# Output projection and second norm of the last head pair begun inside its attention steps

## The reference

```python
s = einsum('bqhd,bkhd->bhqk', q_c, k_c) * scale + bias      # per chunk of 64, 9-chunk band
p = softmax(where(valid, s, NEG)); o = einsum('bhqk,bkhd->bqhd', p, v_c)
x = x + o @ w_o                                              # 16 heads of 64, width 1024
h = x * rsqrt(mean(x*x) + EPS) * g                           # second norm (ln_ffn)
a = h @ w_up                                                 # 1024 -> 2 * 2816
c = conv_b + sum_j full[:, j:j+T] * conv_w[j]                # causal, width 3
gate, val = split(c); x = x + (silu(gate) * val) @ w_down
```

## Time and profile before

| | us |
|---|---|
| median of 3 runs (2596.01 to 2598.01) | 2596.25 |
| profiled execution, its own time | 2593.85 |
| its span | 2592.3 |
| TensorE busy in the span | 2515.1 (97%) |
| VectorE busy | 1560.4 (60%) |
| ScalarE busy | 877.2 (34%) |
| GpSimd busy | 232.0 (9%) |

### The profile page before, as it was taken

How to read it: one execution, slowest core, us unless ns; L and a number is a source line. 1 busy time by engine, 2 the same in 40 slices (tenths; PEclk the granted TensorE clock), 3 DMA queues, 4 the chain that set the end, 5 groups by cost and what they waited for, 6 DMA issues and landing times.

```text
span 2592.3 us, 44046 instructions
## 1 busy us (share of the span) xinstructions
PE 2515.1 (97%) x16343; PEld 2426.8 (94%) x16343; DVE 1560.4 (60%) x2978; ACT 877.2 (34%) x1647; POOL 232.0 (9%) x521
## 2 busy tenths in 40 slices
PE   7999999998899999999999999999999999999998
PEld 7888888886799999999999899999999999999998
DVE  4566666566766666666666624244666666666666
ACT  5433334434522222233332531233333332222223
POOL 0000000000400000000000421222000000000003
PEclk9999999999899999999999999999999999999999
DMA  6111111110111111111111110111111111111012
GB/s 150 47 35 45 41 48 41 39 34 23 33 49 33 49 49 49 49 49 49 49 49 33 51 49 17 41 43 49 49 49 49 49 49 49 49 37 44 32 49 77
DMA packets 101512, 121.32 MB, mean 47 GB/s; under 512 B 3900, under 2 KB 90084, under 8 KB 101412
## 3 DMA queue, kind: packets, MB, share of 16 engines
q1 hardware_dynamic: 97892, 109.91, 13.2%
q0 software_dynamic: 2864, 7.88, 1.3%
q10 hardware_dynamic: 656, 2.12, 0.2%
HBM read 109.49 MB, written 10.40 MB: 46 GB/s over the span
## 4 chain that ended last, share of the span: by engine, by line
PE 89%; DVE 4%; ACT 3%; POOL 2%; issue 1%; DMA 0%; ACTq 0%; DVEq 0%; POOLq 0%
PE psum L160 26%; PE psum L162 26%; PE psum L161 26%; PE psum L906 3%; PE psum L886 3%; PE psum L871 2%; POOL total L231 2%; PE psum L1708 1%; DVE gx_lo L219 1%; PE psum L779 0%; ACT w_hi L679 0%; ACT conv_t L1392 0%; DVE x L1131 0%; DVE gx_lo L1867 0%; DVE conv_t L1457 0%
## 5 line engine op out<-in xcount | busy, mean ns | idle before, releaser
L160 PE MATMUL psum<-gx_hi,w_hi 128*128 128x352 f32 x3264 | 1069.4, 328 | 22.9 <-DVE w_lo L1282 10.6
L161 PE MATMUL psum<-gx_lo,w_hi 128*128 128x352 f32 x3264 | 1058.1, 324 | 0.0
L162 PE MATMUL psum<-gx_hi,w_lo 128*128 128x352 f32 x3264 | 1057.5, 324 | 0.0
L160 PEld LDWEIGHTS psum<-gx_hi,w_hi 128*128 128x128 f32 x3264 | 617.4, 189 | 29.7 <-issue 13.3
L161 PEld LDWEIGHTS psum<-gx_lo,w_hi 128*128 128x128 f32 x3264 | 617.7, 189 | 0.9 <-issue 0.7
L162 PEld LDWEIGHTS psum<-gx_hi,w_lo 128*128 128x128 f32 x3264 | 617.4, 189 | 0.0
L1484 DVE TENSOR_TENSOR x<-x,psum 128x352 f32<-128x352 f32 x528 | 259.1, 518 | 122.3 <-PE psum L162 122.3
L1392 ACT ACTIVATE conv_t<-a_gate,cur 128x352 f32<-128x352 f32 x132 | 90.2, 683 | 534.7 <-DVE a_gate L1449 534.4
L160 PE MATMUL psum<-h_hiA,w_hi 128*128 128x352 f32 x528 | 172.7, 327 | 4.3 <-DVE x L1484 4.3
L160 PE MATMUL psum<-h_hiB,w_hi 128*128 128x352 f32 x528 | 172.7, 327 | 0.0
L162 PE MATMUL psum<-h_hiB,w_lo 128*128 128x352 f32 x528 | 172.2, 326 | 0.0
(11 more groups left out here) (187 smaller groups left out, 3233.1 us busy)
## 6 DMA issues: line engine op xcount, KB each, us to landing
raw<-in_f_w_up SPq DMA_DIRECT2D x44, 1024.0 KB, 5.1
raw<-in_f_w_down SPq DMA_DIRECT2D x22, 1024.0 KB, 4.9
raw<-in_a_w_qkv SPq DMA_DIRECT2D x24, 512.0 KB, 3.8
raw<-in_b_w_in SPq DMA_DIRECT2D x8, 1024.0 KB, 5.8
raw<-in_a_w_o SPq DMA_DIRECT2D x8, 512.0 KB, 3.6
raw<-in_b_w_out SPq DMA_DIRECT2D x4, 1024.0 KB, 5.2
out<-raw SPq DMA_DIRECT2D x6, 512.0 KB, 2.7
xin<-in_x_prompt SPq DMA_DIRECT2D x4, 512.0 KB, 8.4
```

The costliest lines, as they stand in the source:

```text
L160: pe.matmul(out, w[0], rhs[0], start=first, stop=False)
L161: pe.matmul(out, w[0], rhs[1], start=False, stop=False)
L162: return pe.matmul(out, w[1], rhs[0], start=False, stop=last)
```

## The change

- The first six pairs are written out in place of the loop, on every engine.
- The maxima of the two heads are two reductions, and each exponential waits for its own.
- In the last pair all 24 tiles of the pair before stand in passes 0 to 3, and the last pair's own 24 in passes 5 to 10 (`LATE_WO` gives for each pass the tiles ahead of and behind the middle of it). Passes 0 to 3 use banks 7 and 3 in turn, passes 4 to 8 bank 7 alone, passes 9 and 10 four banks.
- In passes 4 and 5 the first gate unit of the FFN is split; from pass 6 on tiles of the second norm are done in the passes (`NORM_TILES`).
- `rstd` comes in two parts (blocks 0 to 3; the rest), in functions of their own. The first FFN iteration of the first layer takes its first six items as (0,0), (1,0), (0,1), (1,1), (0,2), (1,2) in (u, c).
- Buffers are laid out anew so that the FFN's first value weights can be loaded once the pair before the last is through.

The diff, cut:

```diff
+    LATE_WO = [(3, 4), (3, 4), (3, 4), (3, 0), (0, 0), (1, 2), (1, 2), (0, 2), (1, 2), (3, 2), (0, 8)]
...
+            LATE_BANK[late_m] = (7, 3)[late_m % 2] if late_s < 4 else 7 if late_s < STEPS else late_m % 4
+    def late_free(m):
+        return max([j for j in range(m) if LATE_BANK[j] == LATE_BANK[m]], default=-1) + 1
+    NORM_TILES = {6: range(0, 2), 7: range(2, 4), 8: range(4, 6), 9: range(6, 10)}
...
+        def late_wo(s, part):
+            for m in late_tiles(s, part):
+                t, n = LAST - 1 + m // BURST, m % BURST
+                at_least(pe, at_added, ADDED0 + BURST * (LAST - 1) + late_free(m))
...
+                wo_tile(pe, n, t, LATE_BANK[m], O_LAST if m >= BURST else O_MAIN)
...
-                if late and s < STEPS:
-                    turn(t, s - 1, third)
-                    if s >= 4:
-                        late_wo(t, s, 0)
-                    late_wo(t, s, 1)
+                if late:
+                    if 4 <= s < STEPS:
+                        late_wo(s, 0)
+                    turn(t, s - 1, third)
+                    late_wo(s, 1)
...
-        with pe.Fori(0, PAIRS // 2 - 1) as j:
-            pair(2 * j, 0)
-            pair(2 * j + 1, 1)
+        for t in range(LAST - 1):
+            pair(t, t % 2)
...
             for h in range(2):
-                if h == 0:
-                    act.wait_ge(max_done, STEPS * t + s + 1)
+                act.wait_ge(max_done, 2 * (STEPS * t + s) + h + 1)
...
+                if late and s == STEPS:
+                    for m in NORM_TILES[s]:
+                        norm.act_tile(act, *divmod(m, KT))
                 if 1 <= s <= STEPS:
                     copy(t, s - 1, range(min(2, len(key_groups(s - 1)))))
...
-        ffn[0].split(act, None, 0, 0)
-        for c in range(NCH):
-            for d in range(KT):
-                norm.act_tile(act, c, d)
+        for m in range(LAST_NORM, 2 * KT):
+            norm.act_tile(act, *divmod(m, KT))
         act.wait_ge(wo_done, 1 + BURST * PAIRS)
+        ffn[0].split(act, None, 0, 1)
+        for d in range(KT):
+            norm.act_tile(act, 2, d)
...
-            dve.tensor_reduce(neg_max[:rows_of(s), :], both_scores(s), AX.XY if n > BANK else AX.X, ALU.max,
-                              negate=True).then_inc(max_done, 1)
+            for h in range(2):
+                dve.tensor_reduce(neg_max[:rows_of(s), h:h + 1], scores_of(s, h), AX.XY if n > BANK else AX.X, ALU.max,
+                                  negate=True).then_inc(max_done, 1)
...
                     scale(t, s)
                     if late:
+                        late_adds(s, 1)
+                        if s == 5:
+                            ffn[0].split(None, dve, 0, 0)
+                        for m in NORM_TILES.get(s - 1, ()):
+                            norm.dve_tile(dve, *divmod(m, KT))
...
+                elif late:
+                    for m, tile in zip(late_tiles(s, 1), range(NORM_TILES[9][0], LAST_NORM + KT)):
+                        add(LAST, m % BURST, LATE_BANK[m])
+                        norm.dve_tile(dve, *divmod(tile, KT))
...
+        def items(self, first):
+            plain = [(u, c) for u in range(4) for c in range(NCH)]
+            if not first or self.layer:
+                return plain
+            return [(u, c) for c in range(NCH) for u in range(2)] + plain[2 * NCH:]
...
+                    if first and self.layer == 0:
+                        if o in (4, 6):
+                            nb_columns(pe, (o - 4) // 2)
+                        elif o in (5, 7):
+                            nb_spreads(pe, ((0,), (1, 2))[(o - 5) // 2])
...
+                    if first and o == 0 and self.layer == 0:
+                        nb_roots(act, 0)
+                        nb_rstd(act, (0,))
+                        act.wait_ge(self.up, 2 * NCH - 1)
+                        self.split(act, None, it, 2)
+                    elif first and o == 2 and self.layer == 0:
+                        nb_roots(act, 1)
+                        nb_rstd(act, (1, 2))
...
+    def raw1_over(engine):
+        engine.wait_ge(pv_done, 2 * STEPS * LAST)
+        engine.wait_ge(kv_turned, KV_FIRST + KV_PAIR * LAST)
+        engine.wait_ge(v_out, 32 * LAST)
```

More of the change, by code:

```diff
@@ new lines, in nb_roots, with nb_spreads @@
+    def nb_roots(act, g):
+        for k, (rows, cut) in enumerate(NB_COLS[g]):
+            act.wait_ge(nb_mean, NB_AT[g + 1])
+            act.activation(rs_col[rows, cut], rs_col[rows, cut], ACT.Sqrt).then_inc(nb_root, 1)
+    def nb_spreads(pe, parts):
+        for j in parts:
+            a, b, n, bank = Norm.SPREAD[j]
+            pe.wait_ge(nb_diag, min(j, 1) + 1)
+            if j == 2:
+                pe.wait_ge(nb_ready, 1)
+            pe.matmul(psum[:, bank, :b - a], ones[:n, :], total[:n, a:b], start=True, stop=True).then_inc(nb_spread, 1)
@@ L283, in build, with nb_rstd @@
+    def nb_rstd(act, parts):
+        for j in parts:
+            a, b, n, bank = Norm.SPREAD[j]
+            act.wait_ge(nb_spread, j + 1)
+            act.activation(rstd[:, a:b], psum[:, bank, :b - a], ACT.Copy).then_inc(nb_ready, 1)
     x_in = [sem(f"x_in{b}") for b in range(NB + 1)]
@@ L975, in pair @@
                     extra_pe(pe, e, 1 - par, 6)
-            if not (at_pair(t, LAST - 1)):
+            if not late and not at_pair(t, LAST - 1):
                 wo_tiles(t, EARLY_WO, BURST)
-        with pe.Fori(0, PAIRS // 2 - 1) as j:
-            pair(2 * j, 0)
-            pair(2 * j + 1, 1)
+        for t in range(LAST - 1):
+            pair(t, t % 2)
         pair(LAST - 1, 0)
@@ L1139, in pair @@
                     if late and s < 4:
[L1140 to L1141 removed]
+                        late_adds(s, 0)
                 if s == 0 and late:
@@ L1508, in iteration @@
                 done = self.done + it
+                last_of = [self.items(first).index((u, NCH - 1)) + 1 for u in range(4)]
                 at_least(pool, self.conv, UP * done)
```

246 lines of the change are left out of this document (139 added, 107 removed).

## The result

| | us |
|---|---|
| changed kernel, median of 20 runs (2597.6 to 2604.4) | 2601.27 |
| kernel before beside it, 20 runs (2591.8 to 2599.9) | 2596.7 |
| ratio, with its 95% interval | 1.0018 [1.0011, 1.0024] |
| profiled execution: span after, before | 2598.2, 2592.3 |

The change makes the kernel 4.6 us slower, 2.9 to 6.2 by the interval. 6.9 were forecast. All medians here are of fast runs (granted clock about 0.99); one run of places_of_before_splits, slow at 2746.1 us and a clock of 0.85, is left out of its median.

The account below looks back on a forecast made before the run. TensorE was taken to bound the kernel, with 89% of the chain that ends last. Terms -6.0 + 9.4 + 7.8 - 12.3 + 7.0 = +5.9, plus 1 for half clock, gave +6.9: median 2603 us, 8-in-10 range 2585 to 2612.

Parts of the forecast that it names:

- pairs written out, maxima: Ordinary pairs: two back-edge waits and a lower clock go, split maxima cost 0; -6.0 us, bounds -7 and 0.
- steps 0 to 3: Last pair's first four steps: third and later tiles wait for adds on VectorE; +9.4 us, bounds +0.7 and +12.
- steps 4 to 8: Last pair: second tile behind scaling waits for an add and holds the next scores; +7.8 us, bounds +3 and +10.
- step 9 to first FFN matmul: End of the last pair: fewer tiles left and gate weights split early; -12.3 us, bounds -14 and -10.
- FFN to tenth item: FFN's first iteration: second inverse and unit-2 split make TensorE wait; +7.0 us, bounds 0 and +10.
- more half clock: TensorE: more stalls of over 2 us bring more half clock; +1 us, bounds 0 and +5.
- Rival 1: Last pair and FFN start: moved tiles are absorbed, adds slip into VectorE's waits; -10, 2586 us; chance 0.24.
- rival 2: FFN's first iteration costs 0 because the second inverse fits between items; -1 in all, 2595 us; chance 0.15.
- Rival 3: As forecast, but waiting steps fall to 1.2 GHz (+5) and GpSimd blocks scaling (+3); 2611 us; chance 0.08.
- Rival 4: Before the FFN: gate weights' split stays behind the norm; 6 us more than forecast, 2609 us; chance 0.02.

Follow-up runs that it names:

- places_of_before_splits: Changed kernel with the last-but-one pair's tiles placed as before, the last pair's in steps 9 and 10, one inverse, unit 2 and 3 splits moved: 2588.6 us, 0.9958.
- before_written_out: The kernel before with its pairs written out, nothing else changed: 2587.5 us, ratio 0.9961 to the kernel before.
- two_one: Changed kernel with late tiles of steps 5 to 8 placed (2,1),(2,1),(1,1),(2,1), one behind the scaling in each: 2594.1 us, ratio 0.9986 to the kernel before.
- rest_late: Changed kernel with no output or norm tiles in steps 4 to 8; the last pair's 24 tiles in steps 9 and 10: 2607.9 us, 1.0035 to the kernel before.
- two_four: Changed kernel with the 24 tiles of steps 0 to 3 placed (2,4) in each step: 2602.9 us, ratio 1.0021 to the kernel before.
- early_unit_3: Changed kernel with the weight split that item ten waits for taken right after item 2 instead of item 6: 2603.2 us, 1.0028 to the kernel before.

## Why the prediction was right

By its own steps, forecast and measured at the marks of one profile each:

| term | forecast | measured |
|---|---|---|
| pairs written out, maxima | -6.0 | -7.9 |
| steps 0 to 3 | +9.4 | +11.2 |
| steps 4 to 8 | +7.8 | +13.0 |
| step 9 to first FFN matmul | -12.3 | -12.3 |
| FFN to tenth item | +7.0 | +5.0 |
| more half clock | +1 | in the rows above |
| behind the tenth item | 0 | -3.1 |
| sum | +6.9 | +5.9 (medians +4.6) |

- **Pairs written out.** The mechanism is shown from both sides. The size was low by 1.9. About 0.8 come from the maxima head by head, 0.14 us a pair (75.91 against 75.77), for which I had taken 0 with a loss as the far bound. My reason, copies that end after the maximum, doesn't hold in every step. In one step of an ordinary pair the first exponential of before_written_out starts 1.21 us after the copies start, and that of the changed kernel 0.97 after:

```profile
346.08 1.09 ACT L1001 ACTIVATE pT<-psum 128x512 f32<-128x512 f32 x2 [0.28 <-PE psum L884]
347.29 0.80 ACT L1011 ACTIVATE pA<-psum,neg_max 128x640 f32<-128x640 f32 x1
```

```profile
345.69 1.09 ACT L1064 ACTIVATE pT<-psum 128x512 f32<-128x512 f32 x2 [0.28 <-PE psum L939]
346.66 0.80 ACT L1073 ACTIVATE pA<-psum,neg_max 128x640 f32<-128x640 f32 x1
```

- **Steps 0 to 3.** The waits before the third and fourth tiles are where I put them (0.9 to 2.3 us each). Of the 1.8 us over my sum 0.5 are the lower clock: it shows in step 0 alone (7.14 us at 0.76; the same step in two_one 6.66 at 1.00). The rest is a sum that was too small, for two_one takes 31.7 us over the same four steps at a clock of 1.00, where I had 30.3.
- **Steps 4 to 8.** Right in place, wait and order, and in two_one's answer; wrong in size. Worked at full clock they came to 37.9 us, and they took 43.1. Steps 4 to 8 took 7.0, 9.7, 9.8, 8.3 and 8.3 us for 5.9, 8.3, 8.3, 8.3 and 7.1, at granted clocks of 0.76, 0.82, 0.83, 0.99 and 0.80: the one at full clock (scores in 1.35 us instead of 2.19) is the one that I had right. As a shortfall 0.84 is 16% of 42.4 us, 6.8. That estimate is an upper bound, since a lower clock costs nothing while TensorE stands, and it covers the 5.2 that were missing. Pairs of runs measure it in part. Step 4 without tiles takes 5.46 us at 1.00 in rest_late. Steps 6 and 7 have the same tiles in two_four, where the clocks are the other way round (two_four's rows first, then the changed kernel's):

```profile
636.85:645.11 8.26, 5.75 (x48) 4.19 (x48) 6.31 (x12) 4.91 (x12) 0.81 (x2) 1.00 0.00 0
645.11:655.00 9.89, 6.84 (x45) 4.70 (x44) 4.75 (x10) 4.91 (x12) 1.65 (x3) 0.83 0.01 2
```

```profile
637.22:647.06 9.84, 7.33 (x49) 5.32 (x48) 6.50 (x12) 4.91 (x12) 0.81 (x2) 0.83 0.00 0
647.06:655.34 8.28, 5.24 (x45) 3.71 (x44) 4.75 (x10) 4.91 (x12) 1.68 (x3) 0.99 0.01 2
```

At full clock either step is my 8.3, and the lower clock adds 1.6 us to it. In steps 5 and 8 no run shows this, and it is argued from the granted clock.
- **Clock in all.** I took +1 with a bound of +5; in steps 0 to 8 it was some 5, of which 0.5 in step 0 and 1.6 each in steps 4 and 6 are measured. Behind them it was higher than before (1.00 and 0.97 against 0.87 and 0.92), worth at most 3.3 and 2.1 us by the same estimate; what of that was gained in time isn't shown. The Trainium skill, page "TensorE: Matmul & The Clock Gate", section "What's actually happening", has activity as what lifts the clock. Three of the four stretches agree with it; at the FFN's start TensorE was busy for less of the time than before (39.66 of 50.00 us against 42.64 of 45.10) and had the higher clock.
- **Step 9 to the FFN.** 12.9 us, as forecast.
- **FFN's start.** First a_gate after 24.0 us for 25.5, the wait before item ten 7.10 for "about 7". The second inverse costs what was said (means 706.69 to the next a_gate 712.09, 5.4 us); the runs add that taking it out alone is worth only 1.5.
- **Behind the tenth item.** I had nothing here. The first down product is a further 1.7 us later than at the tenth item: the 13.3 us from the one to the other ran at 0.86 behind the wait of 7.10, before it was 11.6 us at 1.00, and TensorE was busy all the time in both. From there the unchanged code took 4.8 us less than in before's profile. It varies by 7 us over profiles of the same code, so I give it no cause.

The signs agree less well than the sum. The first FFN matmul was to come at 81 us and came at 88.2, unit 3 at 133 and came at 138.3. At the tenth item the change had cost 9.0 us, where 6.9 were forecast, and behind that stand terms that were off by 2 us one way and by 5 the other. That the sum comes out at +5.9 is in part luck, the 4.8 us of unchanged code above all.

Rival 1 (tiles absorbed) falls with the step marks, rival 2 with the FFN's +5.0. Rival 3's clock half is about right in the steps, and the kernel didn't reach its 2611 us. Its other half wasn't put to the test. GpSimd's sums began when the scaling was over (scalings at 644.88, 653.14 and 661.83, sums at 645.84, 654.12 and 662.81), so the two never ran side by side for more than 0.05 us, and my reading that the norm tiles bring them together was wrong. Rival 4 falls: the gate weights' low half is made at 637.77, and the wait of 6.26 us is gone.

## What to carry to other kernels

A tile that is moved into a step can only be free if the bank that it needs is freed by an instruction that stands ahead of the step's long wait on its engine; even then three in one bank held the scaling up. Look where the freeing instruction is queued, not whether the engine has idle time. A wait that one engine shows before an item names the path behind it, and taking that wait away moves it to the next meeting of the two engines; so find the engine whose whole list of work sets the stage before you reorder. And test a change in parts: here one plain part (-10 us) hid most of what the rest cost (+14 us).

## What the runs showed of the hardware

- The back edge of a loop over five engines cost TensorE 2.40 to 2.46 us without a releaser. Behind the first one the granted clock was 0.98 over 78 us and that pair took 1.1 us more; behind the second it stayed at 1.00.
- TensorE at the lower of its two levels (1.2 GHz) shows in single rows: the eight score matmuls take 1.35 us at full clock, and 1.98 and 2.19 behind waits of 2.08 and 2.29 us. The same code ran at 1.00 in one run and lower in another: step 4 at 0.76 and 0.63 took 1.6 and 2.6 us more, steps 6 and 7 at 0.83 took 1.6 more. After early_unit_3's 9.36 us of idleness the down passes took 0.49 us for the first 3.5 us, then 0.32.
- VectorE's low half of a norm tile (both inputs in SBUF) took 0.57 to 0.58 us clear of GpSimd's sums and mostly 0.82 to 1.27 beside them.
- The same unchanged 1860 us of work took 1855.6 to 1863.0 us, with granted clocks between 0.96 and 0.99 in the stretch from about 1350 to 1700 us.
